# Memory attention: softmax weights of three of four heads turned on VectorE and moved through DRAM, and the last two heads' values later in the first gate chunk

## Chip, cores and metric

The kernel runs on one core of a Trainium2 chip. The metric is the device time of one execution in microseconds, lower is better. A profiled execution gives a trace of every engine: TensorE (PE, with its weight loads PEld), VectorE (DVE), ScalarE (ACT), GpSimd (POOL), SyncE (SP) and the DMA engines.

## The reference

One window-attention block is followed by two layers of a mixer with three branches: latent attention with 8 heads, a short gated convolution, and attention to 256 memory tokens. All is float32, 512 tokens, width 2048. The change lies in the memory branch, once per layer:

```python
z = rmsnorm_2(x, pre_norm_g[l]) @ w_in[l]
q_lat, kv_lat, k_pe, gb, gc, xin, q_mem, gate = split_cols(z)

def memory_attention(q, mem_n, w_mk, w_mv):        # 4 heads of 128 dims, 256 memory tokens
    mk = (mem_n @ w_mk).reshape(b, m, MEM_HEADS, MEM_HEAD_DIM)
    mv = (mem_n @ w_mv).reshape(b, m, MEM_HEADS, MEM_HEAD_DIM)
    sc = jnp.einsum('bshd,bmhd->bhsm', q, mk) * (MEM_HEAD_DIM ** -0.5)
    p = jax.nn.softmax(sc, axis=-1)
    return jnp.einsum('bhsm,bmhd->bshd', p, mv)

y = concat([a_out, c_out, m_out]) * silu(gate)
x = x + rmsnorm_2(y @ w_o[l], post_norm_g[l])
```

## The kernel before

Activations lie with features on the partitions: 16 tiles of 128 features by 512 tokens. The weight matrices come as a long row of chunks, each 128 output features by 2048 inputs (1 MB), in two slots. A chunk is loaded by SyncE, its high part is copied by ScalarE (`split` in the ACT block, line 1147), and its low part is subtracted by VectorE (`split` in the DVE block, line 1599). TensorE multiplies it in `features`: 16 steps k of three passes each (high by high, high by low, low by high), so 48 matmuls of 512 columns. `features` takes `meanwhile`, a list of (k, work): other work that TensorE does ahead of step k. It begins with `begin`, which waits for the chunk's low part.

Each engine has its own queue, written out by hand, and runs it in order; engines meet at semaphores.

The memory heads c = 0 to 3 go with the chunks QM to QM+3, which make the queries. For each head:

- TensorE ends chunk QM+c. ScalarE copies the high part of the queries (`qm_hi`, line 1492), VectorE subtracts for the low part (`qm_lo`, line 2220).
- `scores_mem(c)`: 12 matmuls of 256 columns, ahead of step 3 of the next chunk. For head 3 they stand behind the values of head 2, outside a chunk.
- VectorE takes the maximum (2225) and its negative (2226), ScalarE the exponentials (1497), VectorE the reciprocal (2230) and the scaling of `prob_m` (2232): tokens on the partitions, 4 x 256 columns.
- `turn_mem(c)`: eight transposes of 128x128 on TensorE into PSUM (987), ahead of step 12 of the next chunk.
- ScalarE copies the high part from PSUM (`ptm_hi`, `turned_mem`, 1481), VectorE subtracts for the low part (`ptm_lo`, `ptm_low`, 2205).
- `values_mem(c)`: six matmuls into `ov`, behind the last step of chunk QM+c+1. VectorE copies the result to `g` (`mem_out`, 2214).

Head 3 has its turn and its values in the first chunk of gates, HEAD+1: the turn ahead of step 2, and ahead of step 5 `end_of_memory`, which is the values of head 3 and then `project_pair`, 36 matmuls that complete chunk HEAD for the first head of the latent attention. Behind HEAD+1 come that head's scores (`scores_head`), which need the rotated and split queries and keys (VectorE 2248 to 2280, starting when the pair projection is complete), and the next gate chunk. The weights of the latent heads are already turned by VectorE in 32x32 blocks (2308) and moved through DRAM by SyncE: `move_out` writes `pt2` to `turned2`, `move_in` reads it back in four transfers, one for each quarter of the partitions, in which the blocks change place. The first block's attention does the same with `pt1` (1768, 390, 393). SyncE also issues all weight loads; each waits until the slot's last low part is subtracted.

Of the kernel before, what the change touches and what calls it, by code (L numbers as in the profile page):

```python
# [22 lines left out]
def build(nc, xT, memT, mem, pos, gains, gain_row, sinks, consts, window, w1, w2, out):  # L23
# [102 lines left out]
    SPLIT_AT = (0, 1, 3, 4, 6, 7, 9, 10)  # L126

    SU, TW, TILES = 512, 2048, S // 2
    Q0, Q1 = 2, KT // 2 - 2
    NP = Q1 - Q0 + 1  # L130
    M_FIRST = (2, 3, 0, 1, 4, 5, 6, 7)
# [8 lines left out]
        return slot, l * len(range(slot, ODD, XR)) + (w // XR + 1)  # L140

    turned_dram = nc.dram_tensor("turned", (P, T1), F32, kind="Internal").ap()
    turned2_dram = nc.dram_tensor("turned2", (P, TB * S), F32, kind="Internal").ap()
    residual = nc.dram_tensor("residual", (LAYERS + 1, P, KT * S), F32, kind="Internal").ap()\
        .rearrange("l p c -> p l c")
    ctx = ExitStack()
    with ctx:
        free = [(nc.sbuf_base + 63) // 64 * 64]

        def sb(name, cols, dt=F32, at=None):  # L150

            if at is None:
# [72 lines left out]
        mk_hi, mv_hi, ptm_lo = (sb(n, 2 * S, F32R, at=g0 + (MLA + 2 * i) * 4 * S)  # L225
                                for i, n in enumerate(("mk_hi", "mv_hi", "ptm_lo")))
        ptm_hi = sb("ptm_hi", MB * S, F32R, at=a0 + 4096)
        v_hi = sb("v_hi", S, F32R, at=a0 + 4096)
        v_raw = [sb("v_raw0", S, at=g0 + (KT - 2) * 4 * S), sb("v_raw1", S, at=a0 + 6144)]
        v_lo = [sb("v_lo0", S, F32R, at=g0 + (KT - 2) * 4 * S), sb("v_lo1", S, F32R, at=a0 + 6144)]  # L230
# [112 lines left out]
            sem(n) for n in ("turned2", "pt2_out", "pt2_in", "pt2_hi", "pt2_lo", "values2", "tanh2", "gate_b", "y_a", "y_b"))  # L343


        pe_from_one, dve_from_one = (scores1, values1, values2), (y1, om_done, y_a)
        block = ctx.enter_context(nc.Block())

# [2 lines left out]
        def _(sp):  # L351
# [52 lines left out]
            def move_in(no):  # L404
# [3 lines left out]
                for keys in range(QUADS):  # L408
                    sp.dma_start(pt2[keys * BLK:(keys + 1) * BLK, :].rearrange("p (a x) -> p a x", a=QUADS),
                                 turned2_dram.rearrange("(a p) (k x) -> k p a x", a=QUADS, k=QUADS)[keys]).then_inc(pt2_in, 16)  # L410

            def load1(j, i):
                load(chunk1(j, i), w1[:, bass.ds(i * 2 + j, 1), :])

# [7 lines left out]
            for l in range(LAYERS):  # L422
                def load2(p, i=0, stride=0, width=CW):
                    c = chunk2(l, p, i, stride)
                    load(c, w2[:, bass.ds(c.n - N1, 1), 0:width], width)

                load2(0)
                if l == 0:
                    move_first(A)
                load2(1)  # L430
                if l == 0:
                    move_first(B)
                else:
                    move_out(l * MLA)
                    move_in(l * MLA)
                load2(2)
                load2(3)

                for p in range(4, KT):
                    load2(WO + p)  # L440
                load2(MEMORY, width=MW[0])
                sp.wait_ge(chunk_done, pair_of(l, Q1)[0].n + 1)
                for n in range(4):
                    part = tile(M_FIRST[2 * n] // 2, 2 * S)
                    sp.dma_start(m_raw[:, part], memT[:, part]).then_inc(m_in[n], 16)
                load2(MEMORY + 1, width=MW[1])
                for n, width in enumerate(MW):
                    if n >= 2:
                        load2(MEMORY + n, width=width)
                load2(QL)  # L450
                with sp.Fori(0, (HEAD - QL - 1) // 2) as i:
                    load2(QL + 1, i, 2)
                    load2(QL + 2, i, 2)
                for p in range(5):
                    load2(HEAD + p, width=HW[p // 3] if p % 3 == 0 else CW)
                with sp.Fori(0, MLA // 2 - 1) as i:
                    for j in range(2):
                        no = l * MLA + (i * 2 + (j + 1))
                        move_out(no)
                        move_in(no)  # L460
                        load2(HEAD + 3 * j + 5, i, 6)
                        load2(HEAD + 3 * j + 6, i, 6, HW[j])
                        load2(HEAD + 3 * j + 7, i, 6)
                move_out(l * MLA + MLA - 1)
                move_in(l * MLA + MLA - 1)
                load2(HEAD + 3 * MLA - 1)
# [154 lines left out]
        def _(pe):  # L621
# [295 lines left out]
            for l in range(LAYERS):  # L917
# [72 lines left out]
                def values_mem(c):  # L990
                    pe.wait_ge(ptm_done, l * MH + (c + 1))
                    pe.wait_ge(om_done, l * MH + (c + 1))
                    pe.wait_ge(mkv_lo_done, l * 2 + 2)
                    for k in range(MB):
                        w = slice(k * 512 + c * P, k * 512 + (c + 1) * P)
                        ins = passes(ov[0][:, :], mv_hi[:, w], mv_lo[:, w], ptm_hi[:, tile(k)], ptm_lo[:, tile(k)],
                                     k == 0, k == MB - 1)
                    ins.then_inc(values_m, 1)

                features(chunk2(l, QM), h_hi, h_lo)  # L1000
                for c in range(1, MH):
                    features(chunk2(l, QM + c), h_hi, h_lo,
                             meanwhile=[(3, lambda: scores_mem(c - 1)), (12, lambda: turn_mem(c - 1))])
                    values_mem(c - 1)
                scores_mem(MH - 1)

                def product(c, to, at, x, first, last, w_moves=False):
# [43 lines left out]
                def head(i, j, first=False, last=False):  # L1051

                    no = l * MLA + (i * 2 + (j + 1))
                    hc = chunk2(l, HEAD + 3 * j, i, 6)

                    def end_of_memory():
                        pe.wait_ge(ptm_done, l * MH + MH)
                        values_mem(MH - 1)
                        project_pair(hc).then_inc(chunk_done, 1)

                    ins = project(hc, j)
                    if j == 0 and not first:
                        pe.wait_ge(exp2, (no - 1) * TB)
                        ins = project_pair(hc)
                    if not first:
                        ins.then_inc(chunk_done, 1)

                    def values_before():
                        values_head(no - 1, i if j == 1 else i - 1, 1 - j)

                    features(chunk2(l, HEAD + 3 * j + 1, i, 6), h_hi, h_lo,
                             meanwhile=[(2, lambda: turn_mem(MH - 1)), (5, end_of_memory)] if first else [(VALUES_AT[j], values_before)])
                    scores_head(no, i, j)
                    features(chunk2(l, HEAD + 3 * j + 2, i, 6), h_hi, h_lo, last_reader=last)

# [66 lines left out]
        def _(act):  # L1142
# [245 lines left out]
            for l in range(LAYERS):  # L1388
# [87 lines left out]

                act.wait_ge(lat_done, l * 6 + 6)
                def turned_mem(c):
                    act.wait_ge(turned_m, l * MH + (c + 1))
                    for b in range(TB):  # L1480
                        act.activation(ptm_hi[:, :].rearrange("p (k q) -> p k q", k=MB)[:, :, tile(b, P)],
                                       bank(b, MEM).rearrange("p (k q) -> p k q", k=MB), ACT.Copy).then_inc(ptm_hi_done, 1)

                for raw_, hi_ in ((mk, mk_hi), (mv, mv_hi)):
                    act.activation(hi_[:, :], raw_[:, :], ACT.Copy).then_inc(mkv_hi_done, 1)
                for c in range(MH):
                    ch = chunk2(l, QM + c)
                    if c > 0:
                        split(chunk2(l, QM + c + 1))
                        turned_mem(c - 1)  # L1490
                    multiplied(ch)
                    act.activation(qm_hi[:, :], acc[ch.slot][:, :], ACT.Copy).then_inc(qm_hi_done, 1)
                    if c == MH - 1:
                        split(chunk2(l, HEAD + 1))
                    act.wait_ge(shift_m, l * MH + (c + 1))
                    for b in range(TB):
                        ins = act.activation(prob_m[:, tile(b, MEM)], bank(b, MEM), ACT.Exp, scale=r_scale[:, b:b + 1],
                                             bias=nm[:, b:b + 1], accum_out=ls[:, b:b + 1])
                    ins.then_inc(exp_m, 1)

                def pt_high(no):
                    act.wait_ge(pt2_in, no * (QUADS * 16))
# [93 lines left out]
        def _(dve):  # L1596
# [470 lines left out]
            for l in range(LAYERS):  # L2067
# [129 lines left out]
                for n, (raw_, hi_, lo_) in enumerate(((mk, mk_hi, mk_lo), (mv, mv_hi, mv_lo))):  # L2197
                    dve.wait_ge(mkv_hi_done, l * 2 + (n + 1))
                    dve.tensor_tensor(lo_[:, :], raw_[:, :], hi_[:, :].bitcast(F32), ALU.subtract).then_inc(mkv_lo_done, 1)

                def ptm_low(c):
                    for b in range(TB):
                        dve.wait_ge(ptm_hi_done, (l * MH + c) * TB + (b + 1))
# [4 lines left out]
                for c in range(MH):  # L2208
# [6 lines left out]

                    if c > 0:
                        split(chunk2(l, QM + c + 1))
                        ptm_low(c - 1)
                    dve.wait_ge(qm_hi_done, no)
                    dve.tensor_tensor(qm_lo[:, :], acc[ch.slot][:, :], qm_hi[:, :].bitcast(F32), ALU.subtract)\  # L2220
                        .then_inc(evacuated[ch.slot], 1)
                    if c > 0:
                        mem_out(c - 1)
                    dve.wait_ge(scores_m, no)
                    link.then(dve.tensor_reduce(mx[:, 0:TB], banks[:, :, 0:MEM], AX.X, ALU.max))
                    dve.tensor_tensor(nm[:, 0:TB], mx[:, 0:TB], r_minus, ALU.mult).then_inc(shift_m, 1)
                    if c == MH - 1:
                        split(chunk2(l, HEAD + 1))
                    dve.wait_ge(exp_m, no)
                    link.then(dve.reciprocal(rl[:, 0:TB], ls[:, 0:TB]))  # L2230
                    for b in range(TB):
                        ins = dve.tensor_scalar(prob_m[:, tile(b, MEM)], prob_m[:, tile(b, MEM)], rl[:, b:b + 1], None, ALU.mult)
                    ins.then_inc(probs_m, 1)

                def pt_low(no):
                    for n in range(2):
# [284 lines left out]
```

## Time and profile before

| | |
|---|---|
| median of 3 runs | 2197.61 us (2196.86 to 2197.83) |
| profiled execution | 2197.51 us, of which the span of the trace is 2195.7 us |
| TensorE busy | 2178.5 us, 99% of the span |
| VectorE busy | 1524.7 us, 69% |
| ScalarE busy | 837.5 us, 38% |
| TensorE transposes of `prob_m` | 64, 32 in each layer |
| granted clock of TensorE | full (0.999 mean) |

The busy time of an engine says how full it is, and the chain that ended last says which engine's work set the end. Here both name TensorE; its waits are few and short, and must be read in the timeline.

### The profile page before, as it was taken

The numbers are of one execution on the slowest core, as the hardware profiler recorded it, in microseconds if no ns is written. First come the engines' busy times: TensorE is split into PE (matmuls) and PEld (weight loads), VectorE is DVE, ScalarE is ACT, GpSimd is POOL, SyncE is SP. The second block draws the span as 40 slices with busy tenths as digits, with TensorE's granted clock in tenths as the row PEclk, the third lists the DMA queues.
The fourth block names the chain that finished last, engine by engine and source line by source line (L and its number), as shares of the span: only waits on it lengthen the run. The fifth ranks groups of instructions, "written<-read, shape, count | busy, mean of one in ns | idle before, by whom it ended". The sixth has DMA issues, their size and how long they took to land.

```text
span 2195.7 us, 27821 instructions
## 1 busy us (share of the span) xinstructions
PE 2178.5 (99%) x10428; PEld 1818.9 (83%) x10428; DVE 1524.7 (69%) x2224; ACT 837.5 (38%) x1307; POOL 211.3 (10%) x215
## 2 busy tenths in 40 slices
PE   8999999999999999999999999999999999999998
PEld 7888888888888888888888888888888888888887
DVE  6677788888988543567677778786434677677665
ACT  6433433453345421334333533444213443435221
POOL 0100000114420100000000053201000000000000
PEclk9999999999999999999999999999999999999999
DMA  7445545442257223225443422573222154435532
GB/s 278 172 154 155 159 157 160 146 149 96 89 213 273 78 96 100 75 75 160 134 139 119 142 107 82 194 268 113 96 96 75 65 158 132 144 117 155 176 119 108
DMA packets 91019, 303.25 MB, mean 138 GB/s; under 512 B 7536, under 2 KB 48752, under 8 KB 67888
## 3 DMA queue, kind: packets, MB, share of 16 engines
q1 hardware_dynamic: 84912, 275.00, 38.0%
q10 hardware_dynamic: 4896, 17.30, 2.1%
q0 software_dynamic: 1120, 9.70, 1.2%
q8 instruction: 61, 1.00, 0.2%
q14 instruction: 30, 0.25, 0.0%
HBM read 253.74 MB, written 48.23 MB: 138 GB/s over the span
## 4 chain that ended last, share of the span: by engine, by line
PE 98%; DMA 1%; DVE 1%; issue 0%; ACT 0%; SPq 0%; DVEq 0%; POOLq 0%; POOL 0%; ACTq 0%
PE acc L631 69%; PE sc L631 11%; PE ov L631 6%; PE sc L855 3%; PE sc L856 2%; PE ov L795 1%; PE sc L782 1%; PE sc L781 1%; PE sc L1038 1%; PE sc L1037 1%; DMA g<-xT_dram 0%; PE acc L816 0%; PE acc L817 0%; PE acc L647 0%; PE acc L820 0%
## 5 line engine op out<-in xcount | busy, mean ns | idle before, releaser
L631 PE MATMUL acc<-h_all,hi 128*128 128x512 f32 x4160 | 1286.9, 391 | 8.9 <-DVE h_all L1691 8.9
L631 PEld LDWEIGHTS acc<-h_all,hi 128*128 128x128 f32 x4160 | 775.6, 188 | 170.5 <-issue 12.0
L631 PE MATMUL acc<-h_all,lo 128*128 128x512 f32 x2080 | 809.9, 389 | 0.0
L1599 DVE TENSOR_TENSOR lo<-raw,hi 128x2048 fp32r<-128x2048 f32 (+3 forms) x158 | 345.1, 2184 | 171.3 <-ACT hi L1147 169.2
L631 PEld LDWEIGHTS acc<-h_all,lo 128*128 128x128 f32 x2080 | 390.8, 188 | 81.9
L1147 ACT ACTIVATE hi<-raw 128x2048 fp32r<-128x2048 f32 (+3 forms) x158 | 289.1, 1830 | 430.5 <-PE acc L631 263.8
L1229 ACT ACTIVATE prob<-prob,st 128x256 f32<-128x256 f32 x128 | 63.6, 498 | 109.4 <-DVE st L1752 109.4
L631 PE MATMUL sc<-hi,h_all 128*128 128x512 f32 (+1 forms) x320 | 90.7, 369 | 0.0
L1306 ACT ACTIVATE hi<-raw 128x512 fp32r<-128x512 f32 x50 | 30.4, 627 | 120.7 <-PE sc L856 107.5
L631 PEld LDWEIGHTS sc<-hi,h_all 128*128 128x128 f32 x320 | 58.1, 189 | 10.4 <-issue 0.5
L1542 ACT ACTIVATE prob<-sc,st 128x512 f32<-128x512 f32 x64 | 44.2, 690 | 43.6 <-DVE st L2299 43.6
L496 POOL TENSOR_TENSOR sqacc<-sqacc,sq 128x512 f32<-128x512 f32 x28 | 53.4, 1907 | 57.9 <-ACT sq L1161 56.4
L631 PE MATMUL sc<-lo,h_all 128*128 128x512 f32 (+1 forms) x160 | 58.8, 368 | 0.0
L1154 ACT ACTIVATE hi<-raw 128x1024 fp32r<-128x1024 f32 x32 | 32.2, 1054 | 68.4 <-PE acc L631 54.3
L855 PE MATMUL sc<-t_parts,hi 128*128 128x512 f32 x160 | 57.8, 398 | 0.0
L2238 DVE TENSOR_TENSOR pt_low<-pt,pt_hi 128x1024 fp32r<-128x1024 f32 x32 | 37.8, 1222 | 25.8 <-ACT pt_hi L1504 25.8
L555 POOL TENSOR_TENSOR t_raw<-g 128x512 f32<-128x512 f32 x4 | 7.1, 1778 | 484.8 <-DVE lo L1599 484.8
L1504 ACT ACTIVATE pt_hi<-pt 128x1024 fp32r<-128x1024 f32 x32 | 32.1, 1052 | 48.4 <-DMA pt<-turned 48.4
L2298 DVE TENSOR_REDUCE st<-sc 128x1 f32<-128x512 f32 x64 | 44.1, 689 | 7.6 <-PE sc L1038 5.1
L1161 ACT ACTIVATE sq<-g 128x512 f32<-128x512 f32 x64 | 38.7, 627 | 22.5 <-POOL qacc L500 7.6
L608 POOL DMA_DIRECT2D cs<-gain_row_dram x1 | 0.6, 623 | 481.6 <-ACT h_all L1164 481.6
L2362 DVE STREAM_TRANSPOSE x_rows<-x_piece 32x512 f32<-32x512 f32 x64 | 45.0, 703 | 2.6 <-DMA x_piece<-residual 0.8
(331 smaller groups left out, 3399.3 us busy)
## 6 DMA issues: line engine op xcount, KB each, us to landing
raw<-w_dram SPq DMA_DIRECT2D x170, 1024.0 KB, 4.9
turned<-pt SPq DMA_DIRECT2D x32, 512.0 KB, 3.2
pt<-turned SPq DMA_DIRECT2D x64, 256.0 KB, 5.1
turned<-pt SPq DMA_DIRECT2D x32, 448.0 KB, 3.0
pt<-turned SPq DMA_DIRECT2D x64, 224.0 KB, 4.0
xr<-residual ACTq DMA_DIRECT2D x16, 512.0 KB, 5.2
residual<-g ACTq DMA_DIRECT2D x16, 512.0 KB, 4.7
raw<-w_dram SPq DMA_DIRECT2D x8, 896.0 KB, 6.6
```

The lines of the kernel that those rows point to most:

```text
L496: pool.tensor_tensor(to[:, :], to[:, :], sq[:, tile(slot)], ALU.add).then_inc(added, 1)
L631: ins = pe.matmul(to, a, b, start=first and n == 0, stop=last and n == 2)
L855: pe.matmul(bank(bank_).rearrange("p (s n) -> p s n", s=2), high_, both, start=first and m == 0, stop=end, skip_group_check=True)
L856: ins = pe.matmul(bank(bank_, TILES), low_, both[:, 0, :], start=False, stop=end, skip_group_check=True)
L1147: act.activation(hi[c.slot][:, 0:width], raw[c.slot][:, 0:width], ACT.Copy).then_inc(hi_done, 1)
L1161: act.activation(sq[:, tile(slot)], src, ACT.Square).then_inc(squared, 1)
L1229: act.activation(prob1[:, tile(n, 256)], prob1[:, tile(n, 256)], ACT.Exp, bias=nm[:, n:n + 1], accum_out=ls[:, n:n + 1])
L1542: act.activation(prob2[:, tile(b)], bank(b), ACT.Exp, scale=MLA_SCALE, bias=nm[:, b:b + 1], accum_out=ls[:, b:b + 1]).then_inc(exp2, 1)
L1599: dve.tensor_tensor(lo[c.slot][:, 0:width], raw[c.slot][:, 0:width], hi[c.slot][:, 0:width].bitcast(F32), ALU.subtract).then_inc(lo_done, 1)
L2238: dve.tensor_tensor(keys_half(pt2_low, n), keys_half(pt2, n), keys_half(pt_hi, n).bitcast(F32), ALU.subtract)\
L2298: link.then(dve.tensor_reduce(mx[:, one], bank(b), AX.X, ALU.max))
L2362: dve.transpose(to[:, 4 * c:4 * c + 4, :, a, :], from_[:, :, :, q, :]).then_inc(x_turned, 1)
```

## The change

`MOVED = 3`. For heads 0, 1 and 2 TensorE doesn't transpose. VectorE turns `prob_m` in 32x32 blocks into `ptm_raw` (four transposes of 128x256, `blocks_mem`), SyncE writes that to DRAM and reads it back in four transfers of 128 KB (`move_mem`), ScalarE copies the high part from it (`moved_mem`) and VectorE subtracts in place (`moved_low`; `ptm_lo` is the same memory as `ptm_raw`). `blocks_mem(c)` therefore waits for the values of head c-1. The value matmuls read and write by blocks, as those of the latent heads do.

The places on TensorE change: the values of heads 0 and 1 stand ahead of step 8 of the chunk after the next (QM+2, QM+3), those of head 2 ahead of step 4 of HEAD+1; head 3 is still turned by TensorE, ahead of step 5 of HEAD+1 (was 2), and `end_of_memory` stands ahead of step 8 (was 5). The output copies of VectorE follow. On SyncE the moves stand ahead of the loads of HEAD, HEAD+1 and HEAD+2.

```diff
 # SyncE
+            def move_mem(no):
+                sp.wait_ge(blocks_m, no + 1)
+                sp.dma_start(turned_m_dram, ptm_raw[:, :]).then_inc(ptm_out, 16)
+                sp.wait_ge(ptm_out, no * 16 + 16)
+                for keys in range(QUADS):
+                    sp.dma_start(ptm_raw[keys * BLK:(keys + 1) * BLK, :].rearrange("p (a x) -> p a x", a=QUADS),
+                                 turned_m_dram.rearrange("(a p) (k x) -> k p a x", a=QUADS, k=QUADS)[keys]).then_inc(ptm_in, 16)
...
                 for p in range(5):
+                    if p < MOVED:
+                        move_mem(l * MOVED + p)
                     load2(HEAD + p, width=HW[p // 3] if p % 3 == 0 else CW)
 # TensorE
                 for c in range(1, MH):
-                    features(chunk2(l, QM + c), h_hi, h_lo,
-                             meanwhile=[(3, lambda: scores_mem(c - 1)), (12, lambda: turn_mem(c - 1))])
-                    values_mem(c - 1)
+                    between = [(3, lambda: scores_mem(c - 1))]
+                    if 0 <= c - 2 < MOVED:
+                        between.append((8, lambda: values_mem(c - 2)))
+                    if c - 1 >= MOVED:
+                        between.append((12, lambda: turn_mem(c - 1)))
+                    features(chunk2(l, QM + c), h_hi, h_lo, meanwhile=between)
+                    if c - 1 >= MOVED:
+                        values_mem(c - 1)
                 scores_mem(MH - 1)
...
-                             meanwhile=[(2, lambda: turn_mem(MH - 1)), (5, end_of_memory)] if first else [(VALUES_AT[j], values_before)])
+                             meanwhile=[(4, lambda: values_mem(MH - 2)), (5, lambda: turn_mem(MH - 1)), (8, end_of_memory)] if first else [(VALUES_AT[j], values_before)])
 # ScalarE
+                def moved_mem(c):
+                    act.wait_ge(ptm_in, (l * MOVED + c + 1) * (QUADS * 16))
+                    act.activation(ptm_hi[:, :], ptm_raw[:, :], ACT.Copy).then_inc(ptm_hi_done, TB)
...
                     act.activation(qm_hi[:, :], acc[ch.slot][:, :], ACT.Copy).then_inc(qm_hi_done, 1)
+                    if 0 <= c - 1 < MOVED and c < MH - 1:
+                        moved_mem(c - 1)
...
                     ins.then_inc(exp_m, 1)
+                moved_mem(MH - 2)
 # VectorE
+                def blocks_mem(c):
+                    dve.wait_ge(values_m, l * MH + c)
+                    to = ptm_raw[:, :].rearrange("p (a k b i) -> p b k a i", a=QUADS, k=MB, b=TB)
+                    for b in range(TB):
+                        ins = dve.transpose(to[:, b], prob_m[:, tile(b, MEM)].rearrange("p (k a j) -> p k a j", k=MB, a=QUADS))
+                    ins.then_inc(blocks_m, 1)
+
+                def moved_low(c):
+                    dve.wait_ge(ptm_hi_done, (l * MH + c + 1) * TB)
+                    dve.tensor_tensor(ptm_lo[:, :], ptm_raw[:, :], ptm_hi[:, :].bitcast(F32), ALU.subtract).then_inc(ptm_done, 1)
...
                     dve.tensor_tensor(nm[:, 0:TB], mx[:, 0:TB], r_minus, ALU.mult).then_inc(shift_m, 1)
+                    if 0 <= c - 1 < MOVED and c < MH - 1:
+                        moved_low(c - 1)
                     if c == MH - 1:
                         split(chunk2(l, HEAD + 1))
                     dve.wait_ge(exp_m, no)
...
                     ins.then_inc(probs_m, 1)
+                    if c == 0 or 0 < c < MOVED:
+                        dve.wait_ge(probs_m, no)
+                        blocks_mem(c)
+                    if 0 <= c - 1 < MOVED and c < MH - 1:
+                        mem_out(c - 1)
+                moved_low(MH - 2)
+                mem_out(MH - 2)
```

## Rows read from the trace of the kernel before

**Rows 1.** The page: span, TensorE's busy time, and the chain that ended last.
```profile
span 2195.7 us, 27821 instructions
...
PE 2178.5 (99%) x10428; PEld 1818.9 (83%) x10428; DVE 1524.7 (69%) x2224; ACT 837.5 (38%) x1307; POOL 211.3 (10%) x215
...
PE 98%; DMA 1%; DVE 1%; issue 0%; ACT 0%; SPq 0%; DVEq 0%; POOLq 0%; POOL 0%; ACTq 0%
```

**Rows 2.** Timeline of TensorE: start us, us, engine, line, operation, out<-in, count.
```profile
904.60 0.61 PE L631 MATMUL acc<-h_all,hi 128*128 128x512 f32 x2
...
917.83 0.39 PE L631 MATMUL ov<-ptm_hi,mv_hi 128*128 128x512 f32 x1
...
965.66 0.63 PE L631 MATMUL acc<-h_all,hi 128*128 128x512 f32 x2
...
973.17 0.39 PE L631 MATMUL sc<-kn_hi,qn_hi 128*128 128x512 f32 x1
```

**Rows 3.** Chain of waits, 940 to 1000 us: start us, us, what.
```profile
943.60 0.87 PE sc L987 x8
...
947.25 0.61 ACT qm_hi L1492
...
947.88 0.70 DVE qm_lo L2220
...
948.63 1.69 PE sc L631 x12
...
998.94 0.07 issue
```

**Rows 4.** Timeline of VectorE, 900 to 1000 us.
```profile
912.26 1.14 DVE L2232 TENSOR_SCALAR prob_m<-prob_m,st 128x256 f32<-128x256 f32 x4
913.86 2.29 DVE L1599 TENSOR_TENSOR lo<-raw,hi 128x2048 fp32r<-128x2048 f32 x1 [0.45 <-ACT hi L1147]
...
926.65 0.18 DVE L2230 RECIPROCAL st<-st 128x4 f32<-128x4 f32 x1 [2.37 <-ACT prob_m L1497]
...
954.35 1.14 DVE L2232 TENSOR_SCALAR prob_m<-prob_m,st 128x256 f32<-128x256 f32 x4
...
972.13 0.68 DVE L2276 TENSOR_TENSOR qr<-rot,qr 64x512 fp32r<-64x512 f32 x1
...
985.26 0.71 DVE L2308 STREAM_TRANSPOSE pt<-prob 128x512 f32<-128x512 f32 x1
```

**Rows 5.** Timeline of ScalarE, 900 to 1000 us.
```profile
924.32 0.56 ACT L1497 ACTIVATE prob_m<-sc,st 128x256 f32<-128x256 f32 x1 [5.69 <-DVE st L2226]
...
996.55 2.01 ACT L1504 ACTIVATE pt_hi<-pt 128x1024 fp32r<-128x1024 f32 x2 [5.17 <-DMA pt<-turned]
```

**Rows 6.** The page's groups: copies and subtractions of 128x1024.
```profile
L2238 DVE TENSOR_TENSOR pt_low<-pt,pt_hi 128x1024 fp32r<-128x1024 f32 x32 | 37.8, 1222 | 25.8 <-ACT pt_hi L1504 25.8
...
L1504 ACT ACTIVATE pt_hi<-pt 128x1024 fp32r<-128x1024 f32 x32 | 32.1, 1052 | 48.4 <-DMA pt<-turned 48.4
```

**Rows 7.** Block transposes by source line: duration ns min/median/max, first and last start.
```profile
L1768 DVE STREAM_TRANSPOSE pt<-prob x32: 1111/1111/1112, 82.6 to 459.0; 128x896 f32<-128x896 f32 x32
...
L2308 DVE STREAM_TRANSPOSE pt<-prob x64: 668/707/715, 982.1 to 2005.6; 128x512 f32<-128x512 f32 x64
```

**Rows 8.** Timeline of SyncE's issues, around 112 us and 989 us.
```profile
111.97 0.51 SPq L390 DMA_DIRECT2D turned<-pt  x1
114.94 1.76 SPq L393 DMA_DIRECT2D pt<-turned  x4
...
989.19 1.76 SPq L409 DMA_DIRECT2D pt<-turned  x4
```

**Rows 9.** Transfers issued at 140.5 to 140.6 us: KB each, us to landing.
```profile
pt<-turned SPq DMA_DIRECT2D x1, 224.0 KB, 3.2
```

**Rows 10.** All transfers in of the first block's attention, line 393: time to landing.
```profile
DMA to landing us min/median/max: 3.0/4.0/5.0
```

**Rows 11.** The page's DMA issues: the heads' transfers in.
```profile
pt<-turned SPq DMA_DIRECT2D x64, 256.0 KB, 5.1
```

More of the change, by code:

```diff
@@ L128, in build @@
     SU, TW, TILES = 512, 2048, S // 2
+    MOVED = 3
     Q0, Q1 = 2, KT // 2 - 2
@@ L142, in build @@
     turned_dram = nc.dram_tensor("turned", (P, T1), F32, kind="Internal").ap()
+    turned_m_dram = nc.dram_tensor("turned_m", (P, TB * MEM), F32, kind="Internal").ap()
     turned2_dram = nc.dram_tensor("turned2", (P, TB * S), F32, kind="Internal").ap()
@@ L227, in build @@
         ptm_hi = sb("ptm_hi", MB * S, F32R, at=a0 + 4096)
+        ptm_raw = sb("ptm_raw", MB * S, at=g0 + (MLA + 4) * 4 * S)
         v_hi = sb("v_hi", S, F32R, at=a0 + 4096)
@@ L343, in build @@
             sem(n) for n in ("turned2", "pt2_out", "pt2_in", "pt2_hi", "pt2_lo", "values2", "tanh2", "gate_b", "y_a", "y_b"))
+        blocks_m, ptm_out, ptm_in = sem("blocks_m"), sem("ptm_out"), sem("ptm_in")
         pe_from_one, dve_from_one = (scores1, values1, values2), (y1, om_done, y_a)
@@ L993, in values_mem @@
                     pe.wait_ge(mkv_lo_done, l * 2 + 2)
+                    to = ov[0][:, :]
+                    if c < MOVED:
+                        to = to.rearrange("p (b a i) -> p a b i", b=TB, a=QUADS)
                     for k in range(MB):
                         w = slice(k * 512 + c * P, k * 512 + (c + 1) * P)
-                        ins = passes(ov[0][:, :], mv_hi[:, w], mv_lo[:, w], ptm_hi[:, tile(k)], ptm_lo[:, tile(k)],
-                                     k == 0, k == MB - 1)
+                        high_, low_ = ptm_hi[:, tile(k)], ptm_lo[:, tile(k)]
+                        if c < MOVED:
+                            high_, low_ = (x[:, :].rearrange("p (a k b i) -> p k a b i", a=QUADS, k=MB, b=TB)[:, k] for x in (ptm_hi, ptm_lo))
+                        ins = passes(to, mv_hi[:, w], mv_lo[:, w], high_, low_, k == 0, k == MB - 1)
                     ins.then_inc(values_m, 1)
@@ L1478, in turned_mem @@
                 def turned_mem(c):
-                    act.wait_ge(turned_m, l * MH + (c + 1))
+                    act.wait_ge(turned_m, l * (MH - MOVED) + (c + 1 - MOVED))
                     for b in range(TB):
@@ L1489, in _ @@
                         split(chunk2(l, QM + c + 1))
-                        turned_mem(c - 1)
+                        if c - 1 >= MOVED:
+                            turned_mem(c - 1)
                     multiplied(ch)
                     act.activation(qm_hi[:, :], acc[ch.slot][:, :], ACT.Copy).then_inc(qm_hi_done, 1)
+                    if 0 <= c - 1 < MOVED and c < MH - 1:
+                        moved_mem(c - 1)
                     if c == MH - 1:
@@ L2217, in _ @@
                         split(chunk2(l, QM + c + 1))
-                        ptm_low(c - 1)
+                        if c - 1 >= MOVED:
+                            ptm_low(c - 1)
                     dve.wait_ge(qm_hi_done, no)
@@ L2221, in _ @@
                         .then_inc(evacuated[ch.slot], 1)
-                    if c > 0:
+                    if c - 1 >= MOVED:
                         mem_out(c - 1)
```

## The prediction

> **What bounds the kernel.** I read the page first: TensorE is busy for 99% of the span, and the chain that ended last lies on it for 98% [rows 1]. So an edit is worth what it takes from TensorE's own queue, less the waits that it opens there. Next I read TensorE's timeline and the chain of waits over one layer's memory attention and first head [rows 2, 3], and beside them the timelines of VectorE and ScalarE [rows 4, 5], to see what would be late next. Times below are on the profile's clock, first layer; the second layer runs the same code on the same sizes, and I give it the same bill.
>
> The unit: 33 matmuls take 7.51 us (965.66 to 973.17) [rows 2], 0.2276 us each, so one step k (three matmuls) is 0.68 us, six matmuls of a value product 1.36 us, a chunk of 48 10.9 us. Chunk QM+1 ran from 904.60 to 917.83 [rows 2]: 13.23 = 10.9 + one turn by TensorE + the scores, which leaves 1.46 us for the scores.
>
> **Removed.** Eight TensorE transposes take 0.87 us of the chain [rows 3]. Three groups go per layer: −2.6 us; both layers −5.2 us. This is all the change can win. ScalarE's four copies of 128x256 become one of 128x1024 (1.05 us), VectorE's four subtractions one of 1.22 us [rows 6]: no loss in either.
>
> **Added on VectorE.** Four block transposes of 128x256 a head. The trace has them at 512 columns (707 ns) and 896 columns (1111 ns) [rows 7]: 1.05 ns a column over 170 ns, so about 440 ns; pipelined as close as the neighbours, 1.4 us for four. For head 0 the weights are scaled by 913.40 (912.26 + 1.14) and the split of QM+2 began at 913.86 [rows 4]. With the transposes between, they end at about 914.87, and the split (2.29 us) ends at 917.12. TensorE, spared the turn, finishes QM+1 at 916.96, and the value product that stood there (1.36 us) has moved away. It waits for the split: **+0.25 us**.
>
> **The round trip, R.** From the last transpose to ScalarE's copy: out through DRAM, SyncE waits, four transfers in of 128 KB. The nearest rows:
> - Out: the attention of the first block sends 448 KB, and the first transfer in is issued 2.97 us after it (111.97 to 114.94) [rows 8]. Here 512 KB in long rows: I take 3.0 us.
> - In: issuing four takes 1.76 us [rows 8], so the last goes 1.3 us after the first. Transfers of 224 KB landed after 3.2 us (the first of a move) up to 5.0 us [rows 9, 10]; the successive landings are about 1.05 us apart. At half the bytes I take half the spacing, 0.6 us, and 2.7 us for the first: the last lands 4.45 us after the first issue; 0.15 us more until ScalarE starts. So R = 3.0 + 4.6 = 7.6 us.
> - Bounds: from below, the issues alone (1.3) and a landing at the quickest seen, 3.0 us or a little under: R about 7.1. From above, if time goes by the number of packets, not by bytes: in the first block 3.0 + 1.3 + 5.0 + 0.15 = 9.5; for the heads' move of 1 MB, ScalarE starts 7.36 us after the first issue (989.19 to 996.55) [rows 5, 8], R = 10.5.
>
> The Trainium skill, "DMA: Bandwidth & Descriptors", section Anatomy of one DMA, gives each transfer about 2.0 us plus its bytes at 436 GB/s (a fit for another issue path). By it each leg is about 3.2 and 2.3 us and R comes to 7.0. The rows disagree with it: the quarters of 224 KB took up to 5.0 us where it gives 2.5.
>
> **Who waits for R.** On ScalarE the copy is queued ahead of the next head's exponentials; on VectorE the low part is ahead of the reciprocal, the scaling, the next transposes, and the next split. Head 0: transposes done 914.87, copy ends 914.87 + 7.6 + 1.05 = T0 = 923.5. VectorE has the low part at T0 + 1.27, TensorE starts the values at T0 + 1.36 = 924.9. TensorE gets to that place (k = 8 of QM+2, begun at 917.2: eight steps 5.45, scores 1.46) at 924.1: **+0.8 us**. From T0 on two chains of the same length lead to QM+3: on TensorE 1.36 + 0.08 + 1.36 + 5.44 = 8.24; on VectorE exponentials 2.33 (924.32 to 926.65) [rows 4, 5], reciprocal and scaling 1.35, transposes 1.48, copy of the output 0.7, split 2.3 = 8.2. Transposes of head 1 end at T0 + 5.16 = 928.7; T1 = 937.3; values at 938.7, which TensorE reaches at 938.65: **+0.05 us**. Each microsecond on R above 7.6 costs two here, one a head. Head 2 has a slack of about 2 us: its copy waits behind the exponentials of head 3 anyway, and the low part is there 0.1 us before TensorE comes: before, VectorE ended the scaling of head 3 at 955.49 (954.35 + 1.14) [rows 4], 5.4 us after those scores (948.63 + 1.5), and the low part adds 1.3; TensorE has 18 projection matmuls (4.1) and four steps (2.7) to do.
>
> **Moved: values of head 2.** Before, they stood between QM+3 and the scores of head 3, and covered the copy and subtraction that make the query parts: ScalarE 947.25, VectorE 947.88, scores at 948.63 [rows 3]. ScalarE starts 0.2 us after a chunk's end (947.05), the six matmuls went on to 948.41, so 0.22 us of wait showed. With the six moved into chunk HEAD+1, the same 1.58 us is bare: **+1.36 us**. The other scores stand three steps (2.04 us) into a chunk, and stay covered.
>
> **Moved: turn and values of head 3, with the pair projection behind them**, by three steps. Everything of the first head starts at the projection's end, E = 965.66: VectorE's rotations and low parts end at 972.81 (972.13 + 0.68) [rows 4], and scores began at 973.17 [rows 2], only 0.36 us later. Three steps fewer behind E bring TensorE there at 971.1, and it waits 1.8 us. That is not regained: the next product of values comes from the same chain (softmax, transposes until 985.97, DRAM), for which TensorE already waited at 998.94 [rows 3, 4]. So what counts is how late E is: three steps more ahead of it, **+2.04 us**.
>
> **Sum per layer**: −2.6 + 0.25 + 0.8 + 0.05 + 1.36 + 2.04 = +1.9; both layers +3.8 us. In terms of R: 2R − 13.3 us per layer, and never under +0.95, when no transfer is waited for. SyncE's loads behind the moves go out some 2 to 4 us later, but are needed more than 10 us after: nothing. The profiled execution took 2197.51 us (span 2195.7 and 1.8 around it), the median is 2197.61; so 2201.5 us.
>
> **Rivals.**
> 1. The transfers are hidden (R up to 7.1): all added waits but those of the fixed order vanish, +0.95 per layer, 2199.5 us. For it: the small pieces and the issue gap of 0.44 us that may keep them apart. This is also where the page's fit would lead.
> 2. Time goes by packets: R 9.5 to 10.5, +5.7 to +7.7 per layer, 2209 to 2213 us. Against it: 224 KB pieces land sooner than 256 KB ones (5.1 us median against 4.0, both cut into as many pieces) [rows 10, 11].
> 3. Between the two, R 8.1 to 8.9: a load issued right behind the moves slows them: 2203.5 to 2206.5 us.
> 4. The other side: faster. If the chain behind E has slack that I don't see (VectorE begins the rotations before the pair projection's last matmul counts, or the next head's values don't wait), the 2.04 falls away; −2.6 + 0.25 + 1.36, no transfer waited for: −1.0 a layer, 2195.5 us. It decides if under 1.0 us of the 2.04 shows and R is under 7.3. Against it: VectorE started at 965.86, right behind E.
>
> The Trainium skill, "VectorE: DVE Perf Modes", section Rules for kernel authors, says to transpose 128x128 on TensorE if PSUM may be the target; its section The three transpose paths says VectorE turns 32x32 blocks only. It speaks against the change; the rows price its side at 0.87 us for eight, against the round trip above, which agrees.
>
> **Chances.** Forecast (2200 to 2203.5) 0.50; rival 1 0.18; rival 2 0.12; rival 3 0.12; rival 4 0.08. I count 0.2% (4.4 us, so 2193.2 and 2202.0) as what a measurement tells from no change. Faster needs nearly the whole 5.2 us: 0.02. Slower: rivals 2 and 3 and a third of the forecast, 0.40. Same: 0.58. The range 2198 to 2207 leaves out rivals 2 and 4.
>
> **What the profile after should show.** 16 TensorE transposes, 24 fewer per layer; 24 VectorE transposes of 128x256 near 440 ns; TensorE waits per layer of 0.3 us before QM+2, about 0.8 at head 0's values, next to none at head 1's, 1.6 before the scores of head 3, 1.8 before the first head's scores. It is wrong if R is far from 7.6 us, or if the first head's scores don't wait.

## The result, and the profile after

The changed kernel takes 2200.14 us (median of 22 runs), the kernel before 2197.23 us in the same sessions: ratio 1.0013, interval 1.0007 to 1.0019. That is +2.9 us, slower and within 0.2%. The forecast was 2201.5 us (+3.9), with a range of 2198 to 2207.

The page of the changed kernel, first the span, the busy times and the chain that ended last, against [rows 1]:

```profile
span 2199.4 us, 27755 instructions
...
PE 2176.2 (99%) x10380; PEld 1814.3 (82%) x10380; DVE 1531.3 (70%) x2230; ACT 836.0 (38%) x1289; POOL 211.3 (10%) x215
...
PE 94%; DVE 3%; DMA 2%; issue 1%; ACT 0%; SPq 0%; POOL 0%; DVEq 0%; POOLq 0%
```

TensorE has 48 instructions less and 2.3 us less of busy time, and the span of this one execution is 3.7 us longer than that of [rows 1] (its time of 2201.25 us is 1.1 over the median): what it was relieved of came back as waits. The chain has 6% that are not TensorE's, where there were 2%. Who TensorE waited for, in the whole execution (us in total, times, longest):

```profile
PE sc L647 <- DVE qr L2331: 3.3, 2, 1.7
PE sc L647 <- DVE qm_lo L2266: 2.8, 2, 1.4
```

These two groups are new; once per layer each. The first is the wait before the first latent head's scores, for the rotated queries; the second is that before the scores of memory head 3. They are the two that come from the places of the work, not from the transfers. Two smaller waits also differ (`pt_low`, 0.3 us where there was none; the split of line 1643, 0.9 where its line 1609 had 0.5); the one for the split is between none and 1.3 us in the traces of the experiments, with no pattern that I can name.

TensorE's timeline, first layer, to be read against [rows 2] and this row of the kernel before, its first scores of head 0:

```profile
906.64 0.28 PE L631 MATMUL sc<-mk_hi,qm_hi 128*128 128x256 f32 x1
```

The rows of the changed kernel are: the first matmul of QM+1, the first scores of head 0, the last step of QM+1 (916.77) and the first of QM+2 (917.62), the values of head 0, the end of the pair projection (the first matmul behind it), the first head's scores.

```profile
905.12 0.62 PE L647 MATMUL acc<-h_all,hi 128*128 128x512 f32 x2
...
907.15 0.28 PE L647 MATMUL sc<-mk_hi,qm_hi 128*128 128x256 f32 x1
...
916.77 0.62 PE L647 MATMUL acc<-h_all,hi 128*128 128x512 f32 x2
917.23 0.39 PE L647 MATMUL acc<-h_all,lo 128*128 128x512 f32 x1
917.62 0.73 PE L647 MATMUL acc<-h_all,hi 128*128 128x512 f32 x2
918.19 0.39 PE L647 MATMUL acc<-h_all,lo 128*128 128x512 f32 x1
...
924.71 0.50 PE L647 MATMUL ov<-ptm_hi,mv_hi 128*128 128x512 f32 x1
...
967.39 0.63 PE L647 MATMUL acc<-h_all,hi 128*128 128x512 f32 x2
...
974.70 0.47 PE L647 MATMUL sc<-kn_hi,qn_hi 128*128 128x512 f32 x1 [1.67 <-DVE qr L2331]
```

From the start of QM+1 to the projection's end it was 61.06 us (904.60 to 965.66) and is 62.27: 1.2 us more, and the second layer shows the same. Both together are 2.4 of the 2.9 us. The wait in front of the first head's scores stands on the last row, 1.67 us. (The profile counts it from the modelled end of the matmul before. From start to start, less the usual 0.23 us, it is 1.85 us, and the 1.41 us before head 3's scores are 1.57. These are the figures to hold against the prediction, which counts from start to start.)

VectorE's timeline, for [rows 4]: the transposes of head 0, the split of QM+2 behind them, and the last low part before the first head's scores.

```profile
913.97 1.42 DVE L2239 STREAM_TRANSPOSE ptm_raw<-prob_m 128x256 f32<-128x256 f32 x4
915.31 2.25 DVE L1633 TENSOR_TENSOR lo<-raw,hi 128x2048 fp32r<-128x2048 f32 x1
...
973.87 0.68 DVE L2331 TENSOR_TENSOR qr<-rot,qr 64x512 fp32r<-64x512 f32 x1
```

The round trip is in SyncE's timeline and then ScalarE's, and the page's issues give the landing times (KB each, us to landing), where [rows 8 to 11] had the nearest ones:

```profile
915.42 0.33 SPq L420 DMA_DIRECT2D turned_m<-ptm_raw  x1
918.04 1.75 SPq L423 DMA_DIRECT2D ptm_raw<-turned_m  x4
```

```profile
922.34 1.06 ACT L1512 ACTIVATE ptm_hi<-ptm_raw 128x1024 fp32r<-128x1024 f32 x1 [4.09 <-DMA ptm_raw<-turned_m]
```

```profile
turned_m<-ptm_raw SPq DMA_DIRECT2D x6, 512.0 KB, 2.6
ptm_raw<-turned_m SPq DMA_DIRECT2D x24, 128.0 KB, 2.8
```

The transposes end at 915.39 (913.97 + 1.42), ScalarE starts at 922.34: R = 6.95 us, 2.65 of them until the first transfer in is issued and 4.30 behind that.

### The profile page after: what moved, and what is told of

It reads as the page before. It is cut to its first block, busy times and chain, and to the rows that moved or that the text cites. A ratio compares the mean times of both kernels' runs of the same rounds, so it can differ in the third digit from the quotient of the medians.

```text
span 2199.4 us, 27755 instructions
## 1 busy us (share of the span) xinstructions
PE 2176.2 (99%) x10380; PEld 1814.3 (82%) x10380; DVE 1531.3 (70%) x2230; ACT 836.0 (38%) x1289; POOL 211.3 (10%) x215
## 4 chain that ended last, share of the span: by engine, by line
PE 94%; DVE 3%; DMA 2%; issue 1%; ACT 0%; SPq 0%; POOL 0%; DVEq 0%; POOLq 0%
PE acc L647 66%; PE sc L647 11%; PE ov L647 6%; PE sc L871 3%; PE sc L872 2%; PE ov L811 1%; PE sc L1064 1%; PE sc L1063 1%; PE sc L798 1%; PE sc L797 1%; DMA raw<-w_dram 1%; DMA pt<-turned 1%; PE acc L832 0%; PE acc L833 0%; PE acc L666 0%
## 5 line engine op out<-in xcount | busy, mean ns | idle before, releaser
L560 POOL COPY vcur<-vall 128x256 f32 x32 | 13.9, 461 | 338.1 <-PE ov L811 337.8
```

## The experiments

The theory: with R near 7 us the trip is hidden, and the change loses by two moves in TensorE's order. The values of head 2 no longer cover the making of head 3's query parts (1.36 us a layer), and the pair projection ends three steps later (2.04 us), behind which all of the first head is a chain on VectorE. The rival: the moves themselves cost (transfers, SyncE's queue), and there is slack where the order changed.

For each run I also read from TensorE's timeline, first layer, the stretch from the first scores of head 0 to the projection's end: 59.02 us before the change (906.64 to 965.66), 60.24 in the changed kernel (907.15 to 967.39). This stretch has a weakness: where an edit moves the projection in TensorE's order (runs 1, 7 and 10), its end moves by construction, whether time is lost or not. For those runs the answer is in what comes behind, the waits and the start of the first latent head's values; the table behind run 10 has that start for all runs.

**1. Only the end of the memory branch later**, in the kernel before:

```diff
-                             meanwhile=[(2, lambda: turn_mem(MH - 1)), (5, end_of_memory)] if first else ...
+                             meanwhile=[(5, lambda: turn_mem(MH - 1)), (8, end_of_memory)] if first else ...
```

> The kernel before, with one edit: the turn of head 3 stands ahead of step 5 of HEAD+1 (was 2), and the values of head 3 with the pair projection ahead of step 8 (was 5). My theory: all that follows in the first head starts at the end of the pair projection, so three steps more ahead of it cost 2.04 us per layer, 4.1 us in all (2201.3 us), and TensorE waits about 1.8 us before the first head's scores. Rival, slack behind the projection: no change (2197.2 us).

Measured: 2201.27 us against 2197.64, ratio 1.0016 (1.0007 to 1.0025); the stretch is 61.09 us, +2.07. TensorE's waits of this run have the line that the changed kernel has:

```profile
PE sc L631 <- DVE qr L2276: 3.4, 2, 1.7
```

Three steps more ahead of the projection make the stretch longer by themselves. That they are not regained is shown behind it: the first latent head's scores start 1.87 us later than before, counted from the first scores of head 0, and its values 2.06 us later (2.09 in the second layer). No transfer was added here and the transposes only changed their place, and the kernel is 3.6 us slower, for 4.1 expected. The term of 2.04 us stands.

**2. Only the values of head 2 out of their place**, in the kernel before:

```diff
                     features(chunk2(l, QM + c), ...)
-                    values_mem(c - 1)
+                    if c < MH - 1:
+                        values_mem(c - 1)
                 scores_mem(MH - 1)
+                values_mem(MH - 2)
...
-                    if c > 0:
+                    if 0 < c < MH - 1:
                         mem_out(c - 1)
...
                     ins.then_inc(probs_m, 1)
+                mem_out(MH - 2)
```

> The kernel before, with the values of head 2 behind the scores of head 3 instead of ahead of them (and their output copy on VectorE behind the scaling of head 3). My theory: the copy and subtraction that make head 3's query parts are bare, TensorE waits 1.58 us instead of 0.22, 1.36 us per layer, 2.7 us in all (2199.9 us). Rival, this wait is taken up by waits that were there behind: no change (2197.2 us).

Measured: 2199.98 us against 2197.64, ratio 1.0012 (1.0003 to 1.0021); the stretch is 60.42 us, +1.40. TensorE's waits:

```profile
PE sc L631 <- DVE qm_lo L2222: 2.8, 2, 1.4
```

The term of 1.36 us stands too.

**3. What a turn is worth in the old order**: one transpose for eight.

```diff
                     for b in range(TB):
                         for k in range(MB):
+                            if c < MH - 1 and (b, k) != (TB - 1, MB - 1):
+                                continue
                             ins = pe.transpose(...)
```

> The kernel before, with one TensorE transpose instead of eight for heads 0, 1 and 2: seven eighths of the turn are left out (their weights are then not turned). It measures what TensorE's turns cost. My theory: seven of eight of 0.87 us, three heads, two layers: 4.6 us less (2192.6 us). Rival: the waits behind the turns (the split, the query parts) take up a part of it, 3 us less or under that (2194.2 us or more).

Measured: 2196.03 us against 2197.64, ratio 0.9992 (0.9983 to 1.0001); the stretch is 58.31 us, −0.71 where I expected −2.3. A miss, and the rival of that expectation holds. The chain of waits of this run, 903 to 920 us, tells why:

```profile
907.98 1.23 DVE st L2227
...
909.90 1.84 ACT prob_m L1499 x7
911.74 1.82 ACT hi L1149
...
913.58 2.29 DVE lo L1601
915.87 1.34 DVE ptm_lo L2207 x4
917.21 0.04 issue
917.25 1.67 PE ov L631 x6
```

From the scores of a head to its values there is no TensorE work on the chain any more: maximum, exponentials, the weight chunk's copy and split, and the low part behind them. By the 0.71 us that were won, that chain is about 0.24 us a head shorter than TensorE's own work in the old order, so only that much of a saved turn shows. The later places of the values, in the changed kernel, are what lets a turn be won at all. I had priced the turn from TensorE's side alone.

**4. The turns in the new order**: eight transposes of heads 0 to 2 put back into the changed kernel, into a bank that nobody reads.

```diff
+                def extra_turn(c):
+                    pe.wait_ge(probs_m, l * MH + (c + 1))
+                    for b in range(TB):
+                        for k in range(MB):
+                            pe.transpose(ov[1][:, b * P:(b + 1) * P], prob_m[...], ident)
...
-                    if c - 1 >= MOVED:
-                        between.append((12, lambda: turn_mem(c - 1)))
+                    between.append((12, lambda: extra_turn(c - 1)))
```

> The changed kernel with eight TensorE transposes of heads 0, 1 and 2 put back ahead of step 12, into an unused bank, read by nobody: it prices the removed turns in the new order. My theory: 0.87 us each, 2.6 per layer, less the wait of 0.28 for the split of QM+2 and 0.1 of the next, which they cover: 2.2 us per layer, 4.4 in all over the changed kernel (2204.6 us). Rival, as in the run with one transpose, VectorE's chain to the values takes most of it, 0.7 us per layer: 2201.6 us.

Measured: 2205.09 us against 2197.33, ratio 1.0037 (1.0024 to 1.0050), 5 us over the changed kernel; the stretch is 62.48 us, 2.24 over its 60.24. In the second layer it is 2.9 us, of which about 0.5 are a wait for `ptm_lo` at the values of head 0 that the first layer doesn't have. In this order the turns were worth at least what the sum says.

**5. The trip longer**: the transfer out sent twice.

```diff
-                sp.dma_start(turned_m_dram, ptm_raw[:, :]).then_inc(ptm_out, 16)
-                sp.wait_ge(ptm_out, no * 16 + 16)
+                for n in range(2):
+                    sp.dma_start(turned_m_dram, ptm_raw[:, :]).then_inc(ptm_out, 16)
+                    sp.wait_ge(ptm_out, no * 32 + (n + 1) * 16)
```

> The changed kernel, with the transfer out sent twice in a row (each waited for), so that the round trip is about 2.6 us longer: 9.6 us where the changed kernel has 6.95. My theory: the sum of the prediction, 2R - 13.3 us per layer, 4.6 us more per layer than the changed kernel, shown as waits of TensorE at the values of heads 0 and 1: 2209.4 us. Rival, the trip lies beside other work at this length too: 2200 us.

Measured: 2209.76 us against 2197.33, ratio 1.0057 (1.0042 to 1.0073). R is 9.63 us here (transposes end at 914.99, ScalarE starts at 924.62). The stretch is 64.92 us, 4.68 over the changed kernel, for the expected 4.6. TensorE's waits of 904 to 970 us:

```profile
PE ov L648 <- DVE ptm_lo L2245: 4.2, 2, 2.6
PE sc L648 <- DVE qm_lo L2267: 1.4, 1, 1.4
```

Two waits at values, 2.59 us for head 0 and 1.65 for head 1, in one layer, for a trip 2.68 us longer: two of the three moves are waited for, the third is not. The trip is all but hidden at about 7 us, and what it is longer costs somewhat under double (4.68 for 2.68 us).

The match of the whole time is in part luck, for the second layer has something that nobody had priced. After the wait for head 0's values TensorE's matmuls start 0.43 us apart instead of 0.23:

```profile
1706.88 0.79 PE L648 MATMUL ov<-ptm_hi,mv_hi 128*128 128x512 f32 x1 [2.66 <-DVE ptm_lo L2245]
...
1708.75 0.63 PE L648 MATMUL ov<-ptm_lo,mv_hi 128*128 128x512 f32 x1
1709.18 0.63 PE L648 MATMUL ov<-ptm_hi,mv_lo 128*128 128x512 f32 x1
```

The granted clock is 0.53 from 1706.8 to 1710.4 us, the lower of TensorE's two levels (1.2 of 2.4 GHz), and full again behind that. It costs about 1.5 us over eight matmuls; the next wait is 0.8 us shorter than in the first layer (0.87 for 1.65). In the first layer a wait of 2.59 us left the clock at full.

**6. No trip at all**: ScalarE copies right behind the transposes. The exchange of blocks through DRAM is left out.

```diff
-                    if p < MOVED:
-                        move_mem(l * MOVED + p)
...
-                    act.wait_ge(ptm_in, (l * MOVED + c + 1) * (QUADS * 16))
+                    act.wait_ge(blocks_m, l * MOVED + c + 1)
```

> The changed kernel without the trip through DRAM: ScalarE copies right after the block transposes. It leaves the exchange of blocks out. My theory: the trip is hidden but for about 0.15 us per layer at head 0's values, so 0.3 us less than the changed kernel (2199.8 us), still 2 to 2.5 us over the kernel before. Rival, the transfers cost more than their waits show (contention with the weight loads, SyncE's queue): 2198 us or less.

Measured: 2199.89 us against 2197.33, ratio 1.0013 (1.0003 to 1.0022); the stretch is 60.03 us, 0.21 under the changed kernel. So all 6 MB of added transfers cost about 0.2 us a layer up to the projection (the median is 0.25 us under the changed kernel's, which is inside the noise), and the rest of the loss is there without them.

**7. The pair projection first**, in the changed kernel: the same work, in another order.

```diff
-                        values_mem(MH - 1)
                         project_pair(hc).then_inc(chunk_done, 1)
+                        values_mem(MH - 1)
```

> The changed kernel with the pair projection ahead of the values of head 3 instead of behind them; TensorE's work is the same. My theory: what follows starts at the projection's end, which comes 1.36 us sooner in each layer, and TensorE waits in front of the first head's scores about 0.5 us instead of 1.8: 2.7 us less than the changed kernel (2197.4 us). Rival, only the amount of work on TensorE counts here: no change (2200.1 us).

Measured: 2197.97 us against 2197.37, ratio 1.0000 (0.9991 to 1.0009). The projection ends 58.90 us after the first scores (909.35 to 968.25), 1.34 sooner, as the order makes it. Behind it, the first latent head's values start 1.87 us sooner than in the changed kernel (1.35 in the second layer), and the wait for the rotated queries is down from 3.3 us to this:

```profile
PE sc L647 <- DVE qr L2331: 0.6, 2, 0.3
```

One swap of two neighbours takes back 2.2 of the 2.9 us, for 2.7 expected.

**8 to 10. Two heads instead of three.** Head 2 turned by TensorE again, so that its values may stand ahead of head 3's scores, and the end of the branch where it was:

```diff
-    MOVED = 3
+    MOVED = 2
...
-                             meanwhile=[(4, lambda: values_mem(MH - 2)), (5, lambda: turn_mem(MH - 1)), (8, end_of_memory)] if first else ...
+                             meanwhile=[(2, lambda: turn_mem(MH - 1)), (5, end_of_memory)] if first else ...
...
-                moved_mem(MH - 2)
...
-                moved_low(MH - 2)
-                mem_out(MH - 2)
```

> The changed kernel with two moved heads instead of three: head 2 is turned by TensorE again, its values stand ahead of head 3's scores, and the turn and values of head 3 stand where they did before the change (steps 2 and 5). My theory: two turns are won (1.74 us per layer), the wait for the split of QM+2 (0.25) and about 0.15 at head 0's values are paid, the 1.36 and 2.04 us are not: 1.3 us per layer less than before, 2.7 us in all (2194.5 us). Rival, the moves cost by themselves what the turns free (SyncE's queue, the transfers): 2197 us or more.

Measured: 2195.61 us against 2197.64, ratio 0.9990 (0.9981 to 0.9999); the stretch is 57.83 us, −1.19 where −1.3 was expected. It is faster than both kernels, by a margin near what can be told apart.

Then the values of head 0 one step later, `(9 if c == 2 else 8, ...)`:

> Two moved heads as in the run before, with the values of head 0 ahead of step 9 of QM+2 instead of 8. My theory: the wait at head 0's values, 0.17 us per layer, goes: 0.3 us less than with step 8, 2195.3 us. Rival, the later values push the split of QM+3 by the same time: no difference (2195.6 us).

Measured: 2194.52 us against 2197.33, ratio 0.9988 (0.9979 to 0.9997); the stretch is 57.57 us, 0.26 less. The first layer's trace shows the gain of that size; the times alone would not.

And on top of that the swap of run 7:

> Two moved heads, values of head 0 at step 9, and the pair projection ahead of the values of head 3. My theory: with two heads TensorE has no wait behind the projection but the 0.2 us at the next head's values, so only that is to be had: 0.4 us less, 2194.1 us. Rival, the whole 1.36 us per layer is won here too: 2191.8 us.

Measured: 2194.26 us against 2197.37, ratio 0.9984 (0.9975 to 0.9993). The projection ends after 56.22 us (906.42 to 962.64), 1.35 sooner, and the time hardly moves: 0.3 us from the run before, inside the noise. Here TensorE's own work is the longer of the two chains behind the projection, so its sooner end is no gain. This is the fastest version that I ran, 3.1 us under the kernel before.

**All runs at a common place.** From the first scores of head 0 to the first matmul of the first latent head's values TensorE takes 92.4 us in the kernel before, in either layer. Against that, in us:

| | first layer | second layer | both | medians |
|---|---|---|---|---|
| changed kernel | +1.40 | +1.12 | +2.5 | +2.9 |
| run 1, late end | +2.06 | +2.09 | +4.2 | +3.6 |
| run 2, values of head 2 | +1.44 | +1.20 | +2.6 | +2.3 |
| run 3, one transpose | −0.60 | −0.89 | −1.5 | −1.6 |
| run 4, turns back | +3.52 | +3.77 | +7.3 | +7.8 |
| run 5, longer trip | +5.80 | +6.41 | +12.2 | +12.4 |
| run 6, no trip | +0.82 | +1.16 | +2.0 | +2.6 |
| run 7, projection first | −0.47 | −0.23 | −0.7 | +0.6 |
| run 8, two heads | −1.18 | −1.39 | −2.6 | −2.0 |
| run 9, step 9 | −1.65 | −1.43 | −3.1 | −2.8 |
| run 10, projection first | −1.67 | −1.73 | −3.4 | −3.1 |

The traces, of one execution each, and the medians agree to 0.6 us, but for run 7, where it is 1.3. Executions also differ ahead of the changed code: head 0's first scores start at 906.64 us in the kernel before, at 907.15 in the changed one and at 909.35 in run 7. Terms of a few tenths can be read from a timeline only, not from the times.

## Why the prediction was right, and by how much each term was off

- **Removed turns, −2.6 us per layer.** Right for the new order: 2.24 us with the two waits that the turns cover (run 4, first layer), for 2.2 expected; 2.9 in the second layer. The prediction did not say that the later places of the values are needed for it; in the old order it is 0.71 us (run 3).
- **Wait for the split of QM+2, +0.25.** Measured 0.27: the last matmul of QM+1 starts at 917.23, the first of QM+2 0.39 us later where 0.23 is usual, and the third another 0.11 late. The four transposes took 1.42 us, for 1.4.
- **The round trip, 7.6 us.** This is the mis-sized term: 6.95. The way out took 2.65 (for 3.0), the way in 4.30 (for 4.6), the four transfers landing after 2.8 us in the middle, where I had started from 3.2 and 5.0 us for 224 KB and taken half the bytes as 0.5 us off the first. The fit of the Trainium skill ("DMA: Bandwidth & Descriptors", section Anatomy of one DMA; it is for transfers issued by GpSimd, and these are SyncE's) comes to 7.0 us, next to the measured one, but by two errors that cancel: out 3.2 us by the rule and 2.6 measured, a piece in 2.3 and 2.8.
- **Waits for the trip, +0.8 and +0.05.** With the R measured, 0.65 us shorter, the prediction's own terms come to 0.15 us for head 0 and nothing for head 1. About 0.2 us remained: the values of head 0 start at 924.71, 0.06 us after the steps ahead of them are through, and their next matmul is 0.1 us late; run 6 takes 0.21 us away. That each microsecond on R above that costs two, one a head, was near: for R = 9.63 us the prediction's terms give 2.8 us at head 0 and 2.1 at head 1, and run 5 has 2.75 and 1.81 from start to start.
- **Values of head 2, +1.36**: 1.40 alone (run 2). In the changed kernel the chain of waits has it bare:

```profile
945.55 0.61 ACT qm_hi L1523
946.18 0.70 DVE qm_lo L2266
946.88 0.04 issue
946.92 1.70 PE sc L647 x12
```

- **Projection three steps later, +2.04**: 2.06 alone at the first head's values (run 1), taken back for the most part by an order in which the projection comes first (run 7).
- **The sum**: −2.6 + 0.27 + 0.2 + 1.36 + 2.04 = 1.3 us per layer, 2.5 in all; the stretches show 2.4, the medians 2.9. The half microsecond between is not explained; it is well inside what the interval of the ratio leaves open (1.5 to 4.2 us).
- **The floor** has a slip: without a wait for the trip the prediction's terms add up to +1.05 per layer (−2.6 + 0.25 + 1.36 + 2.04), not to its +0.95, so the first rival's time should have read 2199.7 us, not 2199.5.

So the mechanism was right but for one term that came out near nothing, 0.2 us for 0.85. Of the rivals, the first (the transfers are hidden, 2199.5 us), to which the prediction gave a chance of 0.18, describes that better than the forecast did: R is under its bound of 7.1 us, and the measured median lies between the two times. That the median is in the forecast's own band, from 2200 us, is luck: it is in by 0.14 us, and the terms as measured (2.5 us in all) would have put it at 2199.7 (2197.23 + 2.5). Time by the number of pieces (rival 2) is out: 128 KB in as many pieces, of half the size, landed sooner, 2.8 us against 4.0 and 5.1. The fourth rival, slack behind the projection, is what runs 1 and 7 rule out for a projection three steps later. With two heads the projection is back in its old place, and there a sooner end gains nothing (run 10), because TensorE is not ahead of VectorE's chain. One version is not among the runs: three moved heads with the turn of head 3 and the projection at their old steps 2 and 5. Runs 1 and 2 price the two places only one at a time, in the kernel before.

The Trainium skill, "VectorE: DVE Perf Modes", section Rules for kernel authors, would have 128x128 transposes on TensorE where PSUM may take the result. These runs agree for the third head and not for the first two: two moved heads win 2 to 3 us of 3.5 us of turns.

## What to carry to other kernels

On a full engine, work taken off is worth its time only if nothing is waiting in its shadow: ask for each removed or moved piece which latency it covered, and price that beside it. Where a long chain on another engine starts from one instruction, it is that instruction's place in the order that sets the time, as long as that chain is longer than the work beside it (with two heads it wasn't, and the same swap won nothing that can be told): two neighbours swapped gave back 2.2 of the 2.9 us that the change had lost. And when a change moves several items, move only those whose successor has somewhere to go: the third head, in the places that it was given here, cost more than it freed, the first two did not.

## What the runs showed of the hardware

- A move of 512 KB out and 4 x 128 KB in (these in pieces of 1 KB) takes 6.95 us from the last transpose to the first reader. The time in grows with the bytes, though the number of pieces is the same, and not in proportion: the 128 KB transfers landed after 2.8 us, those of 224 KB after 4.0 and of 256 KB after 5.1 [rows 10, 11] (4.2 and 4.7 in the changed kernel's trace).
- Block transposes of 128x256 took 403 ns in the median (401 to 446) and 1.42 us for four in a row. The two points of [rows 7] had given 440 ns for one.
- Where TensorE takes up work after a wait, its second matmul is about 0.1 us late on top of the wait (917.62 to 918.19, 0.57 us for two matmuls, where the step before took 0.46 for two, 916.77 to 917.23). Short waits cost more than they show.
- A wait of 2.66 us was followed by 3.5 us at a granted clock near half, with matmuls 0.43 us apart; one of 2.59 us, at the same place a layer earlier, was not (run 5). In no other run's trace did TensorE wait so long in the memory branch.
